# One Trainium2 core, a two-layer decoder trunk: the order of work at the norms, at the launch and at the start of the feed-forward output projection

## The chip, the cores and the metric

The kernel runs on 1 core of one Trainium2 chip. The metric is the device time of one execution in microseconds, the median of several runs. The program uses all five engines of the core: PE (TensorE matmul, with its weight loads PEld), DVE (VectorE), ACT (ScalarE), POOL (GpSimd) and SP (SyncE, which issues most DMAs).

## What is computed

256 tokens with 2048 features pass through two layers. Layer 0 has a mixer of a short convolution and a gated delta rule, layer 1 one of sparse attention; every mixer has an input projection ahead of it and an output projection (`w_out`, 2048 x 2048) behind it. The rest is the same in both layers:

```python
def swiglu_ffn(x, w_in, w_out):                     # FFN_HIDDEN = 5632
    gate, up = jnp.split(x @ w_in, 2, axis=-1)
    return (jax.nn.silu(gate) * up) @ w_out

def reference(x, ...):
    for i in range(DEPTH):                          # DEPTH = 2
        y = conv_deltanet_mixer(x, ...) if i % 2 == 0 else nsa_mixer(x, ...)
        x = layer_norm(DEEPNORM_ALPHA * x + y, ln_mix_g[i], ln_mix_b[i])
        x = layer_norm(DEEPNORM_ALPHA * x + swiglu_ffn(x, ffn_w_in[i], ffn_w_out[i]),
                       ln_ffn_g[i], ln_ffn_b[i])
    return x
```

So there are four norms. Norm 0 stands behind layer 0's mixer, norm 1 behind its feed-forward part, norms 2 and 3 likewise in layer 1. Everything is float32.

## The kernel before

**Precision.** Each float32 operand is split in two parts of a shorter format: `hi` is a copy by ACT (line 512 for weights, into `w_hi`), `lo` is the rest, a subtraction by DVE (line 947, into `w_lo`). A product is three matmuls (`passes`, lines 1570 to 1572): hi x hi, hi x lo, lo x hi. The 256 tokens are two tiles of 128, called tile 0 and tile 1 (`t`).

**Weights.** SP loads them in slabs of 1 MB (128 partitions x 2048) into four slots of `raw` (`RAW_SLOTS`). A slab is two halves of 128 x 1024; half `h` is split into slot `h % 4` of `w_hi` and `w_lo` (`HL_SLOTS` = 4). ACT splits half `h` when PE has used half `h - 4` (semaphore `half_used`), DVE follows ACT, and PE waits for `w_lo_ready`. In both queues a call `halves(n)` splits the next n halves; between these calls stands the rest of the engine's work, so the place of each call in the code sets the order. A half carries 12 matmuls of 512 columns in PE's work.

**Input projections** go chunk by chunk: 512 output columns, four slabs, two of the eight PSUM banks as accumulators, in alternating pairs (banks 0 and 1, banks 2 and 3). The feed-forward part has 22 such chunks, gates and ups in turn. The other four banks, 4 to 7, hold transposes. `up` (DVE, line 1119) multiplies gate and up into `hid`, `hidden_T` (PE, line 1747) transposes it, `put_hT` (ACT, line 620) copies it to `hT`.

**Output projections** (`outer`, in all three engines) use all eight banks as accumulators, 4 columns blocks x 2 tiles of tokens. They go over the k-tiles, 128 rows of the weight each: 16 for `out0` and `out1`, 44 for `fout0` and `fout1`. A k-tile needs two halves of weight and one column of the source, split into `a_hi` (ACT, line 543) and `a_lo` (DVE, line 993). Since every bank is needed from the first k-tile on, PE waits at the start of `fout` for the last `hid`, its transposes and their copies. The last two k-tiles are done bank by bank, first the four banks of tile 0, then those of tile 1, each reported by `bank_whole`.

**The norms** (`ln`). DVE adds each finished bank to `x` and takes its statistics (`moments`, lines 1013 and 1014), ACT takes the root (line 560), DVE inverts (lines 1022, 1027), ACT normalises `x` in two pieces of 128 x 1024 (line 567). PE transposes 512 features at a time (`x_tile_T`, line 1701; q is the quarter, 0 to 3), DVE scales quarters 0 and 2 (`turned_y`, line 1037), ACT quarters 1 and 3 (line 577); ACT splits off `xt_hi` (line 584), DVE `xt_lo` (line 1045, `turned_lo`). The next chunk, PE's `head`, can then begin: in it tile 0 takes the first two slabs alone, then tile 1, and the last two slabs go for both tiles together. The last norm (`last_ln`) writes its results to DRAM (lines 1092, 1093) and ends the program.

**The launch.** SP loads `x` (two tiles, 1 MB each), then the first slabs. PE turns `x` into x^T (`xT`, line 1582), 8 banks full of 4 transposes each through four banks, ACT and DVE split it (lines 530, 981), and then the first chunk, z0, begins.

Of the kernel before, what the change touches and what calls it, by code (L numbers as in the profile page):

```python
# [13 lines left out]
F32 = mybir.dt.float32  # L14
F32R = mybir.dt.float32r
# [61 lines left out]
def trunk(nc, x_in, positions, ln_mix_g, ln_mix_b, ln_ffn_g, ln_ffn_b, ffn_w_in, ffn_w_out,  # L77
          hy_w_in, sc_conv_w, dn_conv_w, dn_a_log, dn_dt_bias, dn_norm_w, hy_w_out,
          nsa_w_in, cmp_pos_k, cmp_w1_k, cmp_w2_k, cmp_pos_v, cmp_w1_v, cmp_w2_v, nsa_w_out,
          inv_freq, ln_by_feature, end_positions, out, stop=None):  # L80
# [3 lines left out]
    with ctx:  # L84
# [129 lines left out]

        bank = [ctx.enter_context(nc.psum_tensor(f"bank{n}", [P, 512], F32)) for n in range(8)]
# [13 lines left out]
        x_in_sem, small_in, nsa_in, w2_in = sem("x_in_sem"), sem("small_in"), sem("nsa_in"), sem("w2_in")  # L229
# [26 lines left out]
        uses([("xT", 0, u) for u in range(8)])  # L256
# [82 lines left out]
        def _(sp):  # L339
# [158 lines left out]
        def _(act):  # L498
            h_next = [0]

            def halves(count, i=None, per=0):

                for _ in range(count):
# [3 lines left out]
                    src, slot = half_of(h)  # L507
                    if h % 2 == 0:
                        act.wait_ge(slab_in[h // 2 % RAW_SLOTS], at(16 * (h // 2 // RAW_SLOTS + 1), i, 2 * per))
                    if h >= HL_SLOTS:  # L510
                        act.wait_ge(half_used, at(h - HL_SLOTS + 1, i, per))
                    act.activation(w_hi[:, slot, :], src, ACT.Copy).then_inc(w_hi_ready, 1)  # L512
# [12 lines left out]
            def split_xt(m):  # L525

                for q in range(4):
                    for u in (2 * q, 2 * q + 1):
                        wait_sp(act, ("xT", m, u))
                        ins = act.activation(xt_hi[:, 2 * u:2 * u + 2, :], sp_bank(("xT", m, u))[:, :].rearrange("p (a t) -> p a t", a=2),  # L530
                                             ACT.Copy)
                    ins.then_inc(xt_hi_ready, 1)

            def outer(name, n):
# [9 lines left out]

                def quad(kt, i=None):
                    for j in range(4):
                        if kt + j + 1 < n:
                            split(kt + j + 1, i)

# [1525 lines left out]
```

## Time and profile before

| | |
|---|---|
| median of 3 runs | 2611.42 us (2608.97 to 2611.67) |
| time of the profiled execution | 2611.9 us |
| span of the profiled execution, first to last instruction | 2610.1 us |
| PE busy, of the span | 2474.3 us, 95% |
| PEld / DVE / ACT busy | 81% / 56% / 44% |
| mean granted TensorE clock | 0.975 of full speed |

A row of a group gives the line, engine and operation, output<-inputs with their shape, the count, then busy time and the mean of one, then idle time before it and what ended it. A row of a timeline gives the start, the duration (of all that the row merges), the instruction, and in brackets the idle time before it. A window gives the busy time and count of each engine, then the granted clock as a share of full speed, which is 2.4 GHz; its lower level is 1.2 GHz. Matmuls overlap: one of 512 columns lasts 0.39 us and the next starts 0.23 us after it.

### The profile page before, as it was taken

How to read it: one execution, taken by the hardware profiler on the slowest of the kernel's cores; microseconds unless marked ns; L12 is line 12 of the kernel's file. 1: busy time of each engine (PE TensorE's matmuls, PEld its weight loads, DVE VectorE, ACT ScalarE, POOL GpSimd, SP SyncE). 2: the span in 40 equal slices, each digit the busy share in tenths (PEclk: the TensorE clock that was granted, in tenths of full speed). 3: DMA queues.
4: the chain of work that ended last, by engine and by line, in shares of the span. 5: the costliest groups of instructions: out<-in, count | busy, mean ns of one | idle time of the engine just before them, and what ended most of it. 6: DMA issues, size and time to landing. Idle time of an engine off the chain costs nothing. (4 is left out here: it accounts for less than half of the span.)

```text
span 2610.1 us, 33820 instructions
## 1 busy us (share of the span) xinstructions
PE 2474.3 (95%) x12841; PEld 2115.6 (81%) x12841; DVE 1452.5 (56%) x1791; ACT 1137.8 (44%) x1498; POOL 25.3 (1%) x71
## 2 busy tenths in 40 slices
PE   7999989888999999999979999979899999999997
PEld 6999979777888888788869877767688888878885
DVE  4666776566444444455567656645754444444556
ACT  4445542345444444444454445534544444444442
POOL 1000000100000000000000000000000000000000
PEclk9999999899999999999999999979999999999998
DMA  7555520344555555555535652215355555565552
GB/s 232 175 187 182 178 81 1 117 159 164 187 197 177 194 192 193 194 193 192 193 119 190 227 176 97 81 67 193 130 192 193 190 182 191 182 208 191 193 193 95
DMA packets 176306, 435.81 MB, mean 167 GB/s; under 512 B 7040, under 2 KB 19440, under 8 KB 159584
## 3 DMA queue, kind: packets, MB, share of 16 engines
q1 hardware_dynamic: 174496, 425.75, 48.7%
q0 software_dynamic: 1728, 8.92, 0.9%
q8 instruction: 57, 0.93, 0.1%
q14 instruction: 25, 0.20, 0.0%
HBM read 432.54 MB, written 2.10 MB: 167 GB/s over the span
## 5 line engine op out<-in xcount | busy, mean ns | idle before, releaser
L947 DVE TENSOR_TENSOR w_lo<-raw,w_hi 128x1024 fp32r<-128x1024 f32 x804 | 978.7, 1225 | 993.7 <-ACT w_hi L512 992.0
L512 ACT ACTIVATE w_hi<-raw 128x1024 fp32r<-128x1024 f32 x804 | 848.5, 1061 | 1130.5 <-PE bank L1572 1119.9
L1570 PE MATMUL bank<-w_hi,xt_hi 128*128 128x512 f32 x1728 | 683.6, 396 | 33.9 <-DVE xt_lo L1045 25.9
L1572 PE MATMUL bank<-w_hi,xt_lo 128*128 128x512 f32 x1728 | 676.8, 392 | 0.0
L1571 PE MATMUL bank<-w_lo,xt_hi 128*128 128x512 f32 x1728 | 676.8, 392 | 0.0
L1570 PEld LDWEIGHTS bank<-w_hi,xt_hi 128*128 128x128 f32 x1728 | 327.8, 190 | 102.2 <-DVE xt_lo L1045 27.3
L1570 PE MATMUL bank<-w_hi,a_hi 128*128 128x512 f32 x960 | 380.1, 396 | 17.1 <-DVE w_lo L947 9.6
L1572 PEld LDWEIGHTS bank<-w_hi,xt_lo 128*128 128x128 f32 x1728 | 327.0, 189 | 69.2
L1571 PEld LDWEIGHTS bank<-w_lo,xt_hi 128*128 128x128 f32 x1728 | 328.0, 190 | 66.9
L1571 PE MATMUL bank<-w_lo,a_hi 128*128 128x512 f32 x960 | 378.6, 394 | 0.0
L1572 PE MATMUL bank<-w_hi,a_lo 128*128 128x512 f32 x960 | 378.1, 394 | 0.0
L1570 PE MATMUL bank<-xt_hi,w_hi 128*128 128x256 f32 x928 | 266.9, 288 | 1.4 <-DVE w_lo L947 1.4
L1572 PE MATMUL bank<-xt_hi,w_lo 128*128 128x256 f32 x928 | 263.3, 284 | 0.0
L1571 PE MATMUL bank<-xt_lo,w_hi 128*128 128x256 f32 x928 | 263.2, 284 | 0.0
L1570 PEld LDWEIGHTS bank<-w_hi,a_hi 128*128 128x128 f32 x960 | 183.1, 191 | 58.0 <-DVE w_lo L947 11.3
L1572 PEld LDWEIGHTS bank<-w_hi,a_lo 128*128 128x128 f32 x960 | 183.4, 191 | 39.0
L1571 PEld LDWEIGHTS bank<-w_lo,a_hi 128*128 128x128 f32 x960 | 183.6, 191 | 38.3
L1570 PEld LDWEIGHTS bank<-xt_hi,w_hi 128*128 128x128 f32 x928 | 178.8, 193 | 3.9 <-DVE w_lo L947 2.3
L1571 PEld LDWEIGHTS bank<-xt_lo,w_hi 128*128 128x128 f32 x928 | 178.8, 193 | 2.0 <-issue 1.9
L1572 PEld LDWEIGHTS bank<-xt_hi,w_lo 128*128 128x128 f32 x928 | 178.7, 193 | 0.0
L993 DVE TENSOR_TENSOR a_lo<-big,a_hi 128x256 fp32r<-128x256 f32 x104 | 43.5, 418 | 6.6 <-ACT a_hi L543 6.6
L543 ACT ACTIVATE a_hi<-big 128x256 fp32r (+1 forms) x104 | 41.3, 400 | 0.2
(284 smaller groups left out, 1385.3 us busy)
## 6 DMA issues: line engine op xcount, KB each, us to landing
raw<-in_ffn_w_in_dram SPq DMA_DIRECT2D x176, 1024.0 KB, 5.0
raw<-in_ffn_w_out_dram SPq DMA_DIRECT2D x88, 1024.0 KB, 4.9
raw<-in_hy_w_in_dram SPq DMA_DIRECT2D x57, 1024.0 KB, 5.2
raw<-in_nsa_w_in_dram SPq DMA_DIRECT2D x41, 1024.0 KB, 5.1
raw<-in_hy_w_out_dram SPq DMA_DIRECT2D x16, 1024.0 KB, 4.8
raw<-in_nsa_w_out_dram SPq DMA_DIRECT2D x16, 1024.0 KB, 4.9
raw<-in_cmp_w_k_dram SPq DMA_DIRECT2D x4, 1024.0 KB, 6.0
raw<-in_cmp_w_v_dram SPq DMA_DIRECT2D x4, 1024.0 KB, 5.4
```

What stands on the lines that cost most here:

```text
L512: act.activation(w_hi[:, slot, :], src, ACT.Copy).then_inc(w_hi_ready, 1)
L543: act.activation(a_hi[:, kt % 4, :], s_, ACT.Copy).then_inc(a_hi_ready, 1)
L947: dv.tensor_tensor(w_lo[:, slot, :], src, w_hi[:, slot, :].bitcast(F32), ALU.subtract)\
L993: dv.tensor_tensor(a_lo[:, kt % 4, :], s_, a_hi[:, kt % 4, :].bitcast(F32), ALU.subtract)\
L1570: pe.matmul(dst, l_hi, r_hi, start=start, stop=False, skip_group_check=shared)
L1571: pe.matmul(dst, l_hi, r_lo, start=False, stop=False, skip_group_check=shared)
L1572: return pe.matmul(dst, l_lo, r_hi, start=False, stop=stop, skip_group_check=shared)
```

## The change

It has four parts. (1) **Launch**: a transposed copy of `x` comes in as an input of the program, `x_by_feature`, laid out in DRAM by the host, and is loaded in four quarters of 0.5 MB into `yt`, each ahead of the slab that needs it; ACT and DVE split it by quarters. The transposes of `xT` are gone, and `x` itself is loaded behind the slabs of z1. (2) **Norms**: at the end of every output projection tile 0 is three k-tiles ahead instead of two. Sixteen halves around each norm use eight slots rather than four: two groups of four lie in `spare_hi` and `spare_lo`, in a part of `big` that is free then. Three of the four transposes of tile 0 stand between tile 1's last banks, the next chunk does all four slabs for tile 0 and then all four for tile 1, and DVE's and ACT's orders follow. (3) **`fout`**: k-tiles 0 and 1 are first done for the four banks that are free already (`begin`), ahead of the last transposes, then for the other four. The splits of the source run two k-tiles ahead. (4) **Last norm**: DVE writes the first two results around tile 1's first bank. The accumulators are renumbered (`acc_bank`), and the last trip of DVE's feed-forward loop is written out.

```diff
-        HEAD = ("ffn0", "vs", "ffn1")
+        HEAD = ("ffn0", "vs", "ffn1", "fout1")
+        OUTER = (("out0", KT), ("fout0", FT), ("out1", KT), ("fout1", FT))
+        TAIL = 3
+        def acc_bank(n, t, c):
+            return pair(C[HEAD[n]] + t)[c] if c < 2 else bank[4 + 2 * t + c - 2]
         def turned_bank(n, t, q):
-            c = C[HEAD[n]]
-            return bank[4 + q] if t else pair(c + 1)[q % 2]
+            return acc_bank(n, 1, q) if t else acc_bank(n, 0, (2, 3, 1, 2)[q])
+        spared = {}
+        for n, (name, kts) in enumerate(OUTER):
+            for p in range(16):
+                spared[2 * (S[name] + kts) - (4 if n % 2 else 5) + p] = (int(n == 2), p)
+        def weights_of(h):
+            where, p = spared.get(h, (0, 4))
+            if p // 4 in (0, 2):
+                return spare_hi[where][:, p % 4, :], spare_lo[where][:, p % 4, :]
+            return w_hi[:, h % HL_SLOTS, :], w_lo[:, h % HL_SLOTS, :]
+        def slot_before(h):
+            if h in spared:
+                return h - 8 if spared[h][1] >= 4 else None
+            return h - HL_SLOTS if h >= HL_SLOTS else None
...
# SP: the launch
+            for quad in range(4):
+                v = slice(4 * quad, 4 * quad + 4)
+                sp.dma_start(yt[:, v, :], x_by_feature[:, v, :]).then_inc(xt_in[quad], 16)
+                slab(S["z0"] + quad, cols(w, quad, slice(6144, 6144 + CH)), as_in)
+            small("ba", w)
+            chunk(S["z1"], w, slice(6144 + CH, 6144 + 2 * CH))
             for t in range(NT):
                 sp.dma_start(x[:, t, :], x_in[0, t * P:(t + 1) * P, :]).then_inc(x_in_sem, 16)
...
# ACT: outer, ln, the end of ffn, the launch
+                ahead = 2 if name[0] == "f" else 1
...
             def ln(n):
+                halves(2)
                 root(n, 0)
+                halves(1)
                 normalise(n, 0)
                 act.wait_ge(gb_in, 48 * (n + 1))
-                halves(2)
+                halves(1)
                 turned_hi(n, 0, 0)
                 turned_hi(n, 0, 1)
+                halves(1)
+                turned_hi(n, 0, 2)
+                halves(1)
+                turned_hi(n, 0, 3)
+                halves(2)
                 root(n, 1)
-                halves(2)
-                turned_hi(n, 0, 2)
                 normalise(n, 1)
-                turned_hi(n, 0, 3)
...
+                def last_hT():
+                    halves(1)
+                    put_hT(k0 + 20, 40)
...
+                outer(f"fout{layer}", FT, last_hT)
...
+            for q in range(4):
+                act.wait_ge(xt_in[q], 16)
+                act.activation(xt_hi[:, 4 * q:4 * q + 4, :], yt[:, 4 * q:4 * q + 4, :], ACT.Copy).then_inc(xt_hi_ready, 1)
+                halves(2)
...
# DVE: last_ln, the end of ffn
                 inverse(n, 0)
                 result(0, slice(0, D // 2))
+                moments(n, 1, 0)
+                result(0, slice(D // 2, D))
                 for c in range(1, 4):
                     moments(n, 1, c)
-                result(0, slice(D // 2, D))
...
+                def last_up():
+                    up(c0 + 21, k0 + 20, False)
+                    mark().then_inc(gb_free, 1)
+                    halves(1)
+                outer(f"fout{layer}", FT, last_up)
...
# PE: outer's start and end, head
+                def begin(banks, last):
+                    for kt in range(2):
+                        pe.wait_ge(a_lo_ready, A0[name] + kt + 1)
+                        for hf in range(2):
+                            h = 2 * (S[name] + kt) + hf
+                            pe.wait_ge(w_lo_ready, h + 1)
...
+                if last_hidden:
...
+                    begin(free, False)
+                    last_hidden()
+                    pair_read(c - 1)
+                    sp_read(2)
+                    begin([b for b in bank if b not in free], True)
...
-                pe.wait_ge(w_lo_ready, h0 + 4)
                 for t in range(NT):
                     v = slice(t * P, (t + 1) * P)
+                    tile(n - TAIL, [t])
                     for c in range(4):
...
+                        if t and norm < 3:
+                            for q in {1: (0, 1), 2: (2,)}.get(c, ()):
+                                x_tile_T(norm, 0, q)
...
-                x_tile_T(n, 0, 0)
-                x_tile_T(n, 0, 1)
-                tokens_of(0, 0)
-                x_tile_T(n, 0, 2)
-                tokens_of(0, 1)
                 x_tile_T(n, 0, 3)
-                for q in range(4):
-                    x_tile_T(n, 1, q)
-                tokens_of(1, 0)
-                tokens_of(1, 1)
...
+                for quad in range(4):
+                    tokens_of(0, quad)
+                    if quad >= 2:
+                        x_tile_T(n, 1, 2 * quad - 4)
+                        x_tile_T(n, 1, 2 * quad - 3)
+                for quad in range(4):
+                    tokens_of(1, quad)
```

The order that this makes is shown at two places. The first is DVE at norm 0, from the first bank of tile 1 to the values by which tile 1 is normalised. Before, with `x<-x,bank` and `stats` being one bank's moments, `yt<-bank,lnT` a scaled quarter, `xt_lo` its lower part and `nmr` the value for the normalisation:

```order
L1013 SCALAR_TENSOR_TENSOR x<-x,bank 128x512
L1014 BN_STATS stats<-x 128x6
L1017 BN_AGGR mv<-stats 128x2
L1037 TENSOR_SCALAR yt<-bank,lnT 128x128 x4
L947 TENSOR_TENSOR w_lo<-raw,w_hi 128x1024
L1045 TENSOR_TENSOR xt_lo<-yt,xt_hi 128x4x128
L947 TENSOR_TENSOR w_lo<-raw,w_hi 128x1024
L1045 TENSOR_TENSOR xt_lo<-yt,xt_hi 128x4x128
L1022 RECIPROCAL rstd<-rstd 128x1
L1027 SCALAR_TENSOR_TENSOR nmr<-mv,rstd 128x1
```

These are its last rows, from tile 1's fourth bank on. The same stretch of the change, up to the same two rows at its end (the lines are those of the changed kernel):

```order
L1063 TENSOR_SCALAR yt<-bank,lnT 128x128 x4
L1039 SCALAR_TENSOR_TENSOR x<-x,bank 128x512
L1040 BN_STATS stats<-x 128x6
L980 TENSOR_TENSOR spare_lo_82<-raw,spare_hi_80 128x1024
L1071 TENSOR_TENSOR xt_lo<-yt,xt_hi 128x4x128
L1039 SCALAR_TENSOR_TENSOR x<-x,bank 128x512
L1040 BN_STATS stats<-x 128x6
L1043 BN_AGGR mv<-stats 128x2
L980 TENSOR_TENSOR spare_lo_82<-raw,spare_hi_80 128x1024
L1071 TENSOR_TENSOR xt_lo<-yt,xt_hi 128x4x128
L980 TENSOR_TENSOR spare_lo_82<-raw,spare_hi_80 128x1024
L980 TENSOR_TENSOR w_lo<-raw,w_hi 128x1024
L1048 RECIPROCAL rstd<-rstd 128x1
L1053 SCALAR_TENSOR_TENSOR nmr<-mv,rstd 128x1
```

Tile 1's third and fourth banks now stand between the quarters of tile 0, and four halves (`spare_lo`, `w_lo`) and two more `xt_lo` stand between the last bank and `nmr`, where two and two stood.

The second place is PE at the start of `fout0`, behind the last chunk of the feed-forward loop (banks and buffers numbered). Before, the transposes of `hid` come first:

```order
L1747 MATMUL bank6<-ident_60,yt_58 128x128 x4
L1747 MATMUL bank7<-ident_60,yt_58 128x128 x4
L1570 MATMUL bank0<-w_hi_50,a_hi_55 128x512
L1571 MATMUL bank0<-w_lo_51,a_hi_55 128x512
L1572 MATMUL bank0<-w_hi_50,a_lo_56 128x512
L1570 MATMUL bank4<-w_hi_50,a_hi_55 128x512
```

In the change these are the rows around the same transposes:

```order
L1608 MATMUL bank5<-w_hi_50,a_hi_55 128x512
L1609 MATMUL bank5<-w_lo_51,a_hi_55 128x512
L1610 MATMUL bank5<-w_hi_50,a_lo_56 128x512
L1808 MATMUL bank6<-ident_60,yt_58 128x128 x4
L1808 MATMUL bank7<-ident_60,yt_58 128x128 x4
L1608 MATMUL bank0<-w_hi_50,a_hi_55 128x512
```

Ahead of the transposes stand 24 matmuls on banks 2, 3, 4 and 5, of which the last three are shown, and behind them 24 on banks 0, 1, 6 and 7.

## Rows read from the trace of the kernel before

**Rows 1.** PE's waits, whole span: us in total, times, longest.
```profile
PE bank L1570 <- DVE xt_lo L1045: 25.9, 6, 4.4
PE bank L1570 <- DVE w_lo L947: 21.7, 11, 2.7
...
PE bank L1570 <- DVE a_lo L993: 7.5, 4, 1.9
```

**Rows 2.** Windows: us, busy time of each engine, granted clock, DMA share, GB/s.
```profile
0.00:15.00 15.00, 3.41 (x16) 3.20 (x16) 2.43 (x3) 4.07 (x4) 11.70 (x41) 1.00 0.88 328
15.00:23.00 8.00, 5.82 (x24) 5.34 (x25) 6.42 (x14) 5.55 (x10) 0.00 (x0) 0.57 1.07 309
...
561.00:621.00 60.00, 46.30 (x203) 37.57 (x202) 41.03 (x64) 31.86 (x47) 0.00 (x0) 0.94 0.38 126
1317.00:1379.00 62.00, 48.30 (x208) 39.12 (x208) 44.60 (x68) 32.09 (x47) 0.00 (x0) 0.92 0.36 118
...
1086.00:1106.00 20.00, 16.50 (x64) 13.05 (x63) 8.10 (x12) 7.22 (x11) 1.60 (x3) 0.83 0.68 243
```

**Rows 3.** PE's waits in the window 561 to 621 us, norm 0.
```profile
PE bank L1570 <- DVE xt_lo L1045: 8.6, 2, 4.4
PE bank L1570 <- DVE w_lo L947: 5.1, 2, 2.7
```

**Rows 4.** Timeline of the launch, PE and ACT.
```profile
8.87 3.41 PE L1582 MATMUL bank<-ident,x 128*128 128x128 f32 x16 [8.87 <-DMA x<-in_x_dram]
...
11.50 2.00 ACT L512 ACTIVATE w_hi<-raw 128x1024 fp32r<-128x1024 f32 x2 [9.40 <-DMA raw<-in_hy_w_in_dram]
...
20.51 0.77 PE L1570 MATMUL bank<-w_hi,xt_hi 128*128 128x512 f32 x1
```

**Rows 5.** Timeline of PE at norm 0: the first transposes.
```profile
580.04 1.03 PE L1701 MATMUL bank<-ident,x 128*128 128x128 f32 x8
```

**Rows 6.** Groups of DVE in the window 561 to 621 us: busy us, mean ns.
```profile
L947 DVE TENSOR_TENSOR w_lo<-raw,w_hi 128x1024 fp32r<-128x1024 f32 x14 | 17.0, 1223 | 7.3 <-ACT w_hi L512 7.2
L1014 DVE BATCH_NORM_STATS2 stats<-x 128x6 f32<-128x512 f32 x8 | 5.6, 695 | 0.3
L1045 DVE TENSOR_TENSOR xt_lo<-yt,xt_hi 128x512 fp32r<-128x512 f32 x8 | 5.4, 688 | 6.3 <-ACT xt_hi L584 6.3
L1013 DVE SCALAR_TENSOR_TENSOR x<-x,bank 128x512 f32<-128x512 f32 x8 | 5.4, 672 | 1.8 <-PE bank L1572 1.8
L1037 DVE TENSOR_SCALAR yt<-bank,lnT 128x128 f32<-128x128 f32 x16 | 5.3, 399 | 3.1 <-PE bank L1701 3.1
```

**Rows 7.** Groups of ACT in the window 561 to 621 us.
```profile
L512 ACT ACTIVATE w_hi<-raw 128x1024 fp32r<-128x1024 f32 x14 | 14.6, 1054 | 10.2 <-PE bank L1572 10.2
L577 ACT ACTIVATE yt<-bank,lnT 128x128 f32<-128x128 f32 x16 | 6.0, 452 | 1.8 <-PE bank L1701 1.8
L584 ACT ACTIVATE xt_hi<-yt 128x512 fp32r<-128x512 f32 x8 | 4.9, 628 | 6.8 <-DVE yt L1037 6.7
L567 ACT ACTIVATE x<-x,nmr,rstd 128x1024 f32<-128x1024 f32 x4 | 4.7, 1231 | 1.2 <-DVE nmr L1027 1.2
```

**Rows 8.** Timeline of the start of `fout0`: DVE, then PE, then ACT.
```profile
1082.43 1.23 DVE L947 TENSOR_TENSOR w_lo<-raw,w_hi 128x1024 fp32r<-128x1024 f32 x1 [1.49 <-ACT w_hi L512]
1085.15 1.23 DVE L947 TENSOR_TENSOR w_lo<-raw,w_hi 128x1024 fp32r<-128x1024 f32 x1 [1.49 <-ACT w_hi L512]
1087.00 1.29 DVE L1119 TENSOR_TENSOR yt<-bank,yt 128x512 f32<-128x512 f32 x2 [0.63 <-PE bank L1572]
...
1091.34 0.77 PE L1570 MATMUL bank<-w_hi,a_hi 128*128 128x512 f32 x1 [1.89 <-DVE a_lo L993]
...
1089.04 1.09 ACT L620 ACTIVATE big<-bank 128x512 f32<-128x512 f32 x2 [3.92 <-PE bank L1747]
```

**Rows 9.** Timeline of the end, PE and DVE.
```profile
2581.43 0.50 PE L1570 MATMUL bank<-w_hi,a_hi 128*128 128x512 f32 x1 [2.41 <-DVE w_lo L947]
...
2606.47 0.75 DVE L1093 SCALAR_TENSOR_TENSOR x<-x,rstd,gb 128x512 f32<-128x512 f32 x1
```

More of the change, by code:

```diff
@@ L523, in chunk_in, with outer @@
                 return pair(c)
-            def split_xt(m):
-                for q in range(4):
[L528 to L534, printed above, removed]
+            def outer(name, n, between=None):
                 src = outer_src(name)
@@ L543, in split @@
                     act.activation(a_hi[:, kt % 4, :], s_, ACT.Copy).then_inc(a_hi_ready, 1)
+                ahead = 2 if name[0] == "f" else 1
                 def quad(kt, i=None):
                     for j in range(4):
-                        if kt + j + 1 < n:
-                            split(kt + j + 1, i)
-                        halves(2 if kt + j < n - 2 or i is not None else n - 1 - kt - j, i, 8)
-                split(0)
+                        if kt + j + ahead < n:
+                            split(kt + j + ahead, i)
+                        halves(2 if kt + j < n - 2 or i is not None else (n - 1 - kt - j) * (ahead == 1), i, 8)
+                for kt in range(ahead):
+                    split(kt)
+                if ahead == 2:
+                    between()
                 loop_over(n // 4 - 1, 8, lambda i: quad(0, i))
@@ L994, in split @@
                       .then_inc(a_lo_ready, 1)
+                ahead = 2 if name[0] == "f" else 1
                 def quad(kt, i=None):
                     for j in range(4):
-                        if kt + j + 1 < n:
-                            split(kt + j + 1, i)
-                        halves(2 if kt + j < n - 2 or i is not None else n - 1 - kt - j, i, 8)
-                split(0)
+                        if kt + j + ahead < n:
+                            split(kt + j + ahead, i)
+                        halves(2 if kt + j < n - 2 or i is not None else (n - 1 - kt - j) * (ahead == 1), i, 8)
+                for kt in range(ahead):
+                    split(kt)
+                if ahead == 2:
+                    between()
                 loop_over(n // 4 - 1, 8, lambda i: quad(0, i))
@@ L1069, in ln @@
                 turned_lo(n, 0, 1)
+                turned_y(n, 0, 2)
+                moments(n, 1, 2)
+                halves(1)
+                turned_lo(n, 0, 2)
+                moments(n, 1, 3)
+                halves(1)
+                turned_lo(n, 0, 3)
+                halves(2)
                 scale(n, 1)
-                turned_y(n, 0, 2)
-                halves(2)
-                turned_lo(n, 0, 2)
-                turned_lo(n, 0, 3)
                 turned_y(n, 1, 0)
@@ L1684, in outer @@
                         for k in range(2):
-                            kt, slot = n - 2 + k, (h0 + 2 * k + hf) % HL_SLOTS
+                            kt, h = n - 2 + k, h0 + 2 * k + hf
+                            pe.wait_ge(w_lo_ready, h + 1)
                             pe.wait_ge(a_lo_ready, A0[name] + kt + 1)
-                            ins = passes(bank[4 * t + c][:, :], a_hi[:, kt % 4, v], a_lo[:, kt % 4, v],
-                                         w_hi[:, slot, cols], w_lo[:, slot, cols], False, k == 1)
+                            w = [part_[:, cols] for part_ in weights_of(h)]
+                            ins = passes(acc_bank(norm, t, c)[:, :], a_hi[:, kt % 4, v], a_lo[:, kt % 4, v],
+                                         *w, False, k == 1)
                             if t and c == 1 and k == 0:
```

162 lines of the change are left out of this document (76 added, 86 removed).

## The prediction, made before the change was run

> **What bounds the kernel now.** I read the waits of PE first, since PE is busy for 95% of the span and each engine behind it for 56% at most. Nearly all of what PE waits for outside the two mixers is in four kinds of places. In the whole span its longest sums are for `xt_lo`, for `w_lo` and for `a_lo` [rows 1]. In the window of norm 0 they are 8.6 us for `xt_lo` and 5.1 us for `w_lo`, 13.7 us together [rows 3]; norms 1 and 2 show the same two sums. The windows then show the clock [rows 2]: at norm 0 a granted mean of 0.94 over 60 us. At half speed such a stretch does half its work, so the time lost is the length times what is missing: 60 x 0.06 = 3.4 us (two dips of 3.4 us at 1.2 GHz, each costing 1.7). Norm 1 has 0.92 over 62 us, 5.1 us. Each dip begins behind a wait of PE. The launch is third: the first matmul of a chunk starts at 20.51 us [rows 4]. The start of `fout` is fourth, and the end fifth, where PE's last bank is followed by DVE alone until 2606.47 + 0.75 = 2607.2 us [rows 9].
>
> **Pace.** One half of weight is split every 2.72 us where nothing waits (1082.43 to 1085.15) [rows 8]; that is PE's time for 12 matmuls. Six, a bank with two k-tiles or a half for one tile of tokens, take 1.36 us, a k-tile 5.45 us.
>
> **Part 1, the launch.** Before, 2 MB of `x` have landed at 8.87 us and a third MB, the first slab, at 11.50 us: 2.63 us for a MB [rows 4]. Now the first slab stands behind 0.5 MB instead of 2, and lands 3.95 us earlier, at 7.55. ACT's half takes 1.05 us [rows 7], DVE's 1.22 [rows 6], and x^T's first quarter, which landed before, is split by then. The first matmul starts at about 9.95 us: **10.6 us earlier**. A quarter and a slab are 1.5 MB, 3.95 us of loading, for 5.45 us of PE, so I expect no later wait in z0. `x` itself, 5.3 us of loading, goes behind z1's slabs, and raw slots hold four slabs, 21.8 us of PE: nothing. The transposes' 32 matmuls are inside the 10.6. The clock is less plain. Before, a dip ran to about 22 us, mean 0.57 in the window from 15 to 23 [rows 2], of which 1.6 us hit z0: 0.8 us come back. But the first matmuls may now be slow themselves. The window from 0 to 15 us claims a granted 1.00 [rows 2], yet there 16 transposes took 3.41 us, 0.213 each [rows 4], and 8 of the same kind took 1.03 us, 0.129 each, at norm 0 [rows 5]. I believe the durations and charge z0 one dip, 1.7 us. The part is worth 10.6 + 0.8 - 1.7 = **9.7 us**. The Trainium skill (TensorE: Matmul & The Clock Gate, Part 1: The HAM clock gate) says that "the default state is throttled, and activity releases the throttle". By that rule the charge stands, by the window's 1.00 it would be nothing and the part worth 11.4; no row shows the clock directly before the first matmul.
>
> **Part 2, the norms.** I lay the engines' orders out by hand, time 0 being PE's end of the k-tile n - 4. Durations: a bank's `moments` 0.67 + 0.69, a half 1.22, four `yt` 1.6 busy but 1.3 in a run of them, `xt_lo` 0.69 [rows 6] (0.05 to 0.1 less from start to start); ACT's half 1.05, four `yt` 1.5, `xt_hi` 0.63, a piece of `x` 1.2 [rows 7]; a group of transposes 0.52 [rows 5].
> PE does k-tile n - 3 for tile 0 (2.7) and its four banks (8.2). DVE follows bank by bank, and with the aggregate, ACT's root and the inverse `nmr` is there at 10.7. ACT splits a half and normalises until 12.4 and 13.6. PE is at 13.7 when it has tile 1's second bank, so the first transposes don't wait. With two more banks and two more groups of transposes it is at 18.5, the start of the next chunk. The wait for `w_lo` at the last k-tile (2.4 of the 5.1 us) is gone, as no half there needs a slot that is in use.
> DVE gets tile 1's first bank at 12.5. From there its queue is full: bank, half, `yt`, bank, `xt_lo` to 18.2, just in time for the chunk. Half, `xt_lo`, `yt`, bank, half, `xt_lo` end at 24.4, where PE came at 24.0: a wait of 0.45. The last bank and another half end at 27.1, where PE came at 25.8: 1.35. PE then meets tile 1's transposes at 28.5. Until `nmr` DVE has done 4 banks (5.3), 6 halves (7.1), 2 `yt` (2.5), 4 `xt_lo` (2.5) and small ones (0.5), 17.9 us from 12.5, so 30.4, and ACT's piece ends at 31.7: 3.2. Behind slab 4 and the last transposes (36.5) tile 1's first `xt_lo` waits for a `yt` of quarter 2 that stands ahead of it in DVE's queue: 38.1, 1.6. Nothing waits after that. The sum is **6.6 us of waits for 13.7**; DVE is the bound here now. All of them look like smaller copies of the old ones (which were 2.4 to 4.4 us); I charge one dip of 1.7 us, behind the 3.2.
> Gains: norm 0, 13.7 + 3.4 - 6.6 - 1.7 = 8.8; norm 1, 13.7 + 5.1 - 8.3 = 10.5; norm 2 like norm 0, 8.8. Together **28.1 us**. The bounds: if no wait leads to a dip, 5.1 us more; if every norm keeps its dips and its waits are 3 us longer than laid out, about 14 less. DVE leaves the norm 8 us ahead of PE with four halves more in hand than before; the residual updates that follow cost it 2.4 us each, two halves for each, 4.9 of the 5.45 us that PE gives it. Nothing is charged.
>
> **Part 3, `fout`.** Before, PE waits 1.6 us for `hid` and 1.9 for `a_lo` (7.5 in four waits) [rows 1], and the window has 0.83 over 20 us, 3.4 us [rows 2]: 6.9 each. Now PE has 24 matmuls, 5.45 us, on free banks first. `up` (1.29) and the fourth half (1.22) [rows 8] fit in these. What is left: `a_lo` of k-tile 0 comes about 0.25 us behind the last chunk, since DVE's half of 1085.15 ends at 1086.38 [rows 8] and 0.4 follow; and the second four banks wait for ACT's two copies, 1.09 [rows 8], of which the first starts under the second group of transposes, so 0.85 stay. No dip. 6.9 - 1.1 = 5.8, less 0.1 for slower first matmuls: 5.7 each, **11.4 us**.
>
> **Part 4, the end.** PE's wait of 2.41 us ends at 2581.43 [rows 9]; less the k-tile of 5.45 time 0 is 2573.6, and DVE ends 33.6 later. In the new order tile 0's statistics end at 9.7, the inverse 0.65 later, the first result (two passes of 1.28) at 13.05, then bank, result, three banks, root (21.6) and four results of 1.45: 27.6. **6.0 us.**
>
> **The sum.** 9.7 + 28.1 + 11.4 + 6.0 = 55.2 us off the profiled execution's own time of 2611.9: **2556.7 us**. That execution stands 0.5 us above the median. A measurement of this kernel can tell about 0.2%, 5 us, from no change.
>
> **The rivals.**
> *The clock stays up.* None of the norms' waits brings a dip: 5.1 less, 2551.6 us. For it: the wait of 2.4 us at norm 0 brought none. Against: both of 4.4 did, and mine of 3.2 lies between. 0.15.
> *DVE holds the norms longer.* It has 17.9 us in a row, and ACT's order is fixed too; each item that comes late moves all behind it. With 3 us more per norm and the old number of dips (7 for 3, 6.8 us) it is 2556.7 + 9 + 6.8 = 2572.5. It decides if DVE's items cost 15% more than in the rows of before. 0.15.
> *The launch gains nothing.* The quarters and slabs share the queue badly and the first matmul stays at 20 us: 9.7 more, 2566. The rows speak against it, since DMA moved 328 GB/s there [rows 2]. 0.05.
> *Slower.* In `fout` the splits of the source now stand two k-tiles ahead, and the halves a half more. If that made one split of each k-tile late by a DVE half, 1.22 us, PE would lose it in 88 k-tiles: 107 us, 2664. It decides from 55.2 / 88 = 0.63 us per k-tile on. Against: a freed slot is split in 1.05 + 1.22 and two handovers, 2.5 us, and the half is due 8 us after it was freed. 0.03.
> The forecast has the rest, 0.62.
>
> **Range.** From 2547 us (no dips at the norms, none at the launch, 3 us to spare) to 2572 us, where DVE's case is half in. Faster 0.96, within 0.2% 0.01, slower 0.03.
>
> **What would show it.** PE's first matmul near 10 us; in the norm windows waits for `xt_lo` and `x` near 5 us and for `w_lo` near 1.4, and DVE without idle time for 18 us; at `fout` no wait over 1 us and a granted clock of 1.00; the last result 27.6 us behind k-tile n - 4. A first matmul after 13 us, waits of over 10 us at a norm, or new waits for `w_lo` in the long loops would make it wrong.

## The result, and the profile after

The changed kernel takes **2552.97 us** (median of 4 runs, 2552.24 to 2554.32), the kernel before 2611.55 us beside it (4 runs, 2608.97 to 2611.74). The ratio is 0.9779, with a 95% interval of 0.9762 to 0.9795. The forecast was 2556.7 us, 3.7 us too high. The profiled execution of the change took 2553.14 us, of which its span is 2551.4.

PE's waits over the whole span, after the change (columns as in [rows 1]: us in total, times, longest):

```profile
PE bank L1608 <- DVE w_lo L980: 14.6, 5, 10.4
...
PE bank L1768 <- ACT x L591: 8.2, 3, 2.7
PE bank L1608 <- DVE xt_lo L1071: 5.8, 6, 1.6
...
PE bank L1608 <- DVE a_lo L1015: 4.4, 4, 2.1
...
PE bank L1608 <- DVE spare_lo L980: 3.1, 3, 1.1
```

`xt_lo` has gone from 25.9 to 5.8 us. `w_lo` had 21.7 us in 11 waits; of its 14.6 us now, 10.4 are the launch (before, its longest wait was 2.7). In their place stand the normalised `x` of tile 1 with 8.2 and a half in the spare slots with 3.1 us, one wait at each norm.

To see where the time went, I take PE's start or end at the same matmul in both traces (an end is the last matmul's start plus PE's pace of 0.23 us):

| Place in the program | before | after | gained since the start |
|---|---|---|---|
| z0 ends | 43.17 | 34.43 | 8.74 |
| `out0` starts | 487.56 | 477.33 | 10.23 |
| the first chunk behind norm 0 ends | 620.56 | 600.79 | 19.77 |
| the last chunk ahead of `fout0` ends | 1086.58 | 1066.85 | 19.73 |
| k-tile n - 4 of `fout0` ends | 1317.30 | 1292.32 | 24.98 |
| the first chunk behind norm 1 ends | 1378.36 | 1341.07 | 37.29 |
| `out1` starts | 1745.02 | 1706.28 | 38.74 |
| the first chunk behind norm 2 ends | 1876.75 | 1829.62 | 47.13 |
| the last chunk ahead of `fout1` ends | 2342.78 | 2295.68 | 47.10 |
| k-tile n - 4 of `fout1` ends | 2573.43 | 2521.13 | 52.30 |
| the span ends | 2610.1 | 2551.4 | 58.7 |

So the launch gave 8.7 us, the norms 9.5, 12.3 and 8.4, the starts of `fout` 5.2 each, the end 6.4, and the two mixers, in which PE has the same matmuls as before, 1.5 each.

**The launch.** The eight groups of transposes of `x` are no longer in the timed program: the host lays the transposed copy out. ACT's timeline, then PE's (us from the span's start, duration, instruction, in brackets the wait before it):

```profile
7.97 2.00 ACT L541 ACTIVATE w_hi<-raw 128x1024 fp32r<-128x1024 f32 x2 [2.29 <-DMA raw<-in_hy_w_in_dram]
...
10.43 0.77 PE L1608 MATMUL bank<-w_hi,xt_hi 128*128 128x512 f32 x1 [10.43 <-DVE w_lo L980]
10.99 0.63 PE L1609 MATMUL bank<-w_lo,xt_hi 128*128 128x512 f32 x1
...
15.35 0.40 PE L1608 MATMUL bank<-w_hi,xt_hi 128*128 128x512 f32 x1
15.59 0.40 PE L1609 MATMUL bank<-w_lo,xt_hi 128*128 128x512 f32 x1
```

The first slab lands at 7.97 us, where 7.55 were forecast. Matmuls then start 0.43 us apart (10.99, 11.42, 11.85) until about 14.8, and 0.23 apart from there on: half speed for 4.4 us.

**The windows** at the launch and at norms 0, 1 and 2, then at the start of `fout0` (columns as in [rows 2]):

```profile
0.00:15.00 15.00, 4.57 (x11) 3.64 (x12) 6.79 (x7) 8.24 (x8) 12.59 (x30) 1.00 0.89 322
...
550.00:601.00 51.00, 45.25 (x205) 36.59 (x204) 36.04 (x60) 27.21 (x43) 0.00 (x0) 0.97 0.42 150
1292.00:1342.00 50.00, 44.27 (x211) 35.79 (x210) 41.46 (x65) 28.98 (x45) 0.00 (x0) 1.00 0.47 161
1779.00:1830.00 51.00, 45.26 (x205) 36.60 (x204) 35.90 (x60) 28.54 (x44) 0.00 (x0) 0.97 0.41 149
...
1066.00:1086.00 20.00, 18.99 (x87) 15.35 (x86) 10.79 (x15) 8.68 (x12) 1.59 (x3) 1.00 0.75 288
```

Before, the norms had a granted clock of 0.94 and 0.92 and the start of `fout0` 0.83 [rows 2]. Norms 0 and 2 now have one dip each (581.6 to 585.0 and 1810.4 to 1813.8), norm 1 and `fout0` none.
**Norm 0**, PE's timeline, the four places where it waits:

```profile
574.91 0.50 PE L1608 MATMUL bank<-spare_hi,xt_hi 128*128 128x512 f32 x1 [0.33 <-DVE xt_lo L1071]
...
577.62 0.50 PE L1608 MATMUL bank<-spare_hi,xt_hi 128*128 128x512 f32 x1 [1.05 <-DVE spare_lo L980]
...
582.02 1.97 PE L1768 MATMUL bank<-ident,x 128*128 128x128 f32 x8 [2.75 <-ACT x L591]
...
589.75 0.50 PE L1608 MATMUL bank<-w_hi,xt_hi 128*128 128x512 f32 x1 [1.62 <-DVE xt_lo L1071]
```

Counted as the delay of the next start against PE's own pace, these are 0.49, 1.21, 2.91 and 1.66 us, the same to 0.02 at all three norms; 0.45, 1.35, 3.2 and 1.6 were forecast. The transposes at 582.02 take 1.97 us where the same eight took 1.03 [rows 5]: the dip. DVE's timeline shows its queue from tile 1's first bank to the value for the normalisation:

```profile
563.06 0.69 DVE L1039 SCALAR_TENSOR_TENSOR x<-x,bank 128x512 f32<-128x512 f32 x1 [1.65 <-PE bank L1610]
...
580.34 0.15 DVE L1048 RECIPROCAL rstd<-rstd 128x1 f32<-128x1 f32 x1
580.53 0.16 DVE L1053 SCALAR_TENSOR_TENSOR nmr<-mv,rstd 128x1 f32<-128x1 f32 x1
```

It is 17.6 us long without a gap, from 12.4 to 30.1 us behind k-tile n - 4 (550.62). Forecast: 17.9 us, from 12.5 to 30.4. (Between tile 1's last bank and `nmr` stand three halves and one `xt_lo`, as the list of the changed order has it; the sentence below that list, which says four and two, counts from the third bank.)

**The start of `fout0` and the end**, PE's and DVE's timelines:

```profile
1067.23 0.47 PE L1608 MATMUL bank<-w_hi,a_hi 128*128 128x512 f32 x1 [0.22 <-DVE a_lo L1015]
...
1074.60 0.47 PE L1608 MATMUL bank<-w_hi,a_hi 128*128 128x512 f32 x1 [0.78 <-ACT big L648]
...
2548.22 0.75 DVE L1123 SCALAR_TENSOR_TENSOR x<-x,rstd,gb 128x512 f32<-128x512 f32 x1
```

Two short waits are left at `fout0`. DVE's last result ends at 2548.97, 27.84 us behind k-tile n - 4; 27.6 were forecast.

### The profile page after: what moved, and what is told of

It reads as the page before. It is cut to its first block, busy times and chain, and to the rows that moved or that the text cites. A ratio compares the mean times of both kernels' runs of the same rounds, so it can differ in the third digit from the quotient of the medians.

```text
span 2551.4 us, 33741 instructions
## 1 busy us (share of the span) xinstructions
PE 2450.6 (96%) x12809; PEld 2094.8 (82%) x12809; DVE 1448.5 (57%) x1783; ACT 1134.5 (44%) x1494; POOL 31.0 (1%) x71
## 4 chain that ended last, share of the span: by engine, by line
PE 89%; DVE 8%; ACT 2%; issue 1%; DMA 0%; DVEq 0%; SPq 0%; ACTq 0%
PE bank L1608 27%; PE bank L1609 27%; PE bank L1610 27%; PE bank L1872 3%; PE bank L2064 1%; PE bank L1808 1%; ACT gb L897 1%; DVE w_lo L980 1%; PE bank L2034 1%; DVE stats L1040 1%; PE bank L1861 1%; DVE spare_lo L980 1%; DVE sm L1524 0%; DVE x L1039 0%; DVE yt L1063 0%
## 5 line engine op out<-in xcount | busy, mean ns | idle before, releaser
L980 DVE TENSOR_TENSOR w_lo<-raw,w_hi 128x1024 fp32r<-128x1024 f32 x776 | 943.9, 1224 | 941.3 <-ACT w_hi L541 939.7
L541 ACT ACTIVATE w_hi<-raw 128x1024 fp32r<-128x1024 f32 x776 | 819.2, 1061 | 1064.6 <-PE bank L1610 1059.8
L1608 PE MATMUL bank<-w_hi,xt_hi 128*128 128x512 f32 x1680 | 661.0, 393 | 15.3 <-DVE w_lo L980 10.4
L1610 PE MATMUL bank<-w_hi,xt_lo 128*128 128x512 f32 x1680 | 655.7, 390 | 0.0
L1609 PE MATMUL bank<-w_lo,xt_hi 128*128 128x512 f32 x1680 | 655.5, 390 | 0.0
L1608 PEld LDWEIGHTS bank<-w_hi,xt_hi 128*128 128x128 f32 x1680 | 316.9, 189 | 80.9 <-issue 10.4
L1608 PE MATMUL bank<-w_hi,a_hi 128*128 128x512 f32 x896 | 351.1, 392 | 6.0 <-DVE a_lo L1015 4.4
L1609 PE MATMUL bank<-w_lo,a_hi 128*128 128x512 f32 x896 | 350.5, 391 | 0.0
L1610 PE MATMUL bank<-w_hi,a_lo 128*128 128x512 f32 x896 | 350.4, 391 | 0.0
L1609 PEld LDWEIGHTS bank<-w_lo,a_hi 128*128 128x128 f32 x896 | 169.3, 189 | 35.2
L1015 DVE TENSOR_TENSOR a_lo<-big,a_hi 128x256 fp32r<-128x256 f32 x104 | 43.3, 418 | 13.7 <-ACT a_hi L563 13.7
L639 ACT ACTIVATE yt<-bank 128x512 f32<-128x512 f32 x44 | 23.9, 597 | 43.6 <-PE bank L1610 43.6
```

The source lines that it names most:

```text
L541: act.activation(weights_of(h)[0], half_of(h), ACT.Copy).then_inc(w_hi_ready, 1)
L980: dv.tensor_tensor(lo, half_of(h), hi.bitcast(F32), ALU.subtract).then_inc(w_lo_ready, 1)
L1015: dv.tensor_tensor(a_lo[:, kt % 4, :], s_, a_hi[:, kt % 4, :].bitcast(F32), ALU.subtract)\
L1608: pe.matmul(dst, l_hi, r_hi, start=start, stop=False, skip_group_check=shared)
L1609: pe.matmul(dst, l_hi, r_lo, start=False, stop=False, skip_group_check=shared)
L1610: return pe.matmul(dst, l_lo, r_hi, start=False, stop=stop, skip_group_check=shared)
```

## Experiments

A ratio is against the kernel before, run on the same chip, with its 95% interval. The kernel before took 2609.9, 2609.6 and 2610.3 us (medians) in the three series.

### Which part gives what

**The launch alone.** The kernel before, with the change's launch only:

```
+            for q in range(4):
+                act.wait_ge(xt_in[q], 16)
+                act.activation(xt_hi[:, 4 * q:4 * q + 4, :], yt[:, 4 * q:4 * q + 4, :], ACT.Copy).then_inc(xt_hi_ready, 1)
+                halves(2)
```

> The kernel before with the new launch alone. If the parts are independent and only waits and dips of the clock count, chunk z0 ends 8.7 us earlier, as in the change, and the whole execution is 8.7 us faster (about 2603 us), give or take one or two dips of the clock in the first mixer (1.7 us each), in which the change itself was 1.5 us faster though nothing is edited there. The rival says that the 1.5 us in the mixer come with the launch (x out of the way of the first slabs, another order of loads): then this kernel shows them too, 10.2 us in all at the start of out0.

Measured: 2601.96 us (2596.03 to 2602.53, 6 runs), ratio 0.9968 [0.9955, 0.998], 7.9 us less by the medians. The trace is of the fastest execution, 2596.03 us, while the other five took 2600.4 to 2602.5. In it z0 ends at 33.55 us, 9.6 earlier than before, and `out0` starts 11.5 earlier. The waits for `xt_lo` and `a_lo` are those of before, and those for `w_lo` too, less the launch (10.3):

```profile
PE bank L1575 <- DVE w_lo L950: 31.9, 12, 10.3
PE bank L1575 <- DVE xt_lo L1048: 25.8, 6, 4.4
...
PE bank L1575 <- DVE a_lo L996: 7.5, 4, 1.9
```

So the launch stands by itself and the norms' gain owes nothing to it. Layer 0's mixer takes 1.9 us less here than before and layer 1's 3.8, and no edit accounts for either; the section on the prediction comes back to this.

**`fout`: transposes first, then the free banks.** Only the place of one call differs from the change; the splits stay two k-tiles ahead:

```
-                    begin(free, False)
                     last_hidden()
                     pair_read(c - 1)
                     sp_read(2)
+                    begin(free, False)
                     begin([b for b in bank if b not in free], True)
```

> The change, but in fout PE does the last transposes first and then the same matmuls on the four free banks. The source's first two k-tiles are still split ahead. If the 24 matmuls ahead of the transposes are what hides the chain, PE waits about 1.8 us for hid and 0.8 us for ACT's copies, 2.6 us instead of 1.2, and 1.7 to 3.4 us more from a dip of the clock behind it: 3 to 5 us per fout, 6 to 10 us in all, 2559 to 2563 us. The rival says that splitting the source ahead is what does it (before, the wait for a_lo was the longer one): then it is 1.4 us per fout and no dip, 2556 us.

Measured: 2557.33 us (2556.48 to 2559.73), ratio 0.9799 [0.9782, 0.9815], between what the theory (2559 to 2563) and the rival (2556) expected. PE's waits at `fout0` in this kernel, then the window of `fout1`:

```profile
PE bank L1808 <- DVE yt L1150: 1.8, 1, 1.8
PE bank L1608 <- ACT big L648: 0.8, 1, 0.8
```

```profile
2296.00:2310.00 14.00, 11.46 (x47) 8.99 (x46) 4.12 (x8) 3.23 (x6) 1.58 (x3) 0.88 0.70 290
```

In the trace this costs 1.45 us at `fout0`, where no dip follows, and 3.08 us at `fout1`, where one does (2300.7 to 2304.1). So the rival's 1.4 us came true at `fout0` and the theory's 3 to 5 us at `fout1`. The 24 matmuls ahead of the transposes hide 1.5 us, and 1.6 more where their absence brings a dip. By difference the rest of the 5.2, 3.8 us at `fout0` and 2.1 at `fout1`, belongs to what this kernel keeps. In it the wait for `a_lo` behind the transposes (1.9 us) is gone, ACT's copies (0.8) have appeared, and of the 6.8 us at the lower clock that each start had before, none is left at `fout0` and 3.4 at `fout1`. So most of that rest is dips that don't come, with the splits two k-tiles ahead as the likely reason. Those splits were not run alone.

**The norms: tile 0 two k-tiles ahead, not three.** `tile(n - 3)` is done for both tiles together:

```
-        TAIL = 3
+        TAIL = 2
...
                 tile(n - 4, range(NT))
+                tile(n - 3, range(NT))
...
-                    tile(n - TAIL, [t])
```

> The change with tile 0 two k-tiles ahead instead of three. By the hand-laid schedule the first transposes of tile 0 now wait about 1.6 us for the normalised x in each of three norms, of which 0.6 us is won back from the later wait for w_lo, since DVE is the bound from then on: 0.9 us more per norm, and at the end DVE starts 2.7 us later and ends 2.7 us later: 5.5 us slower in all, about 2558.5 us. The rival says that the third k-tile is what made the norm faster: then it would be over 3 us per norm and over 12 us in all.

Measured: 2556.16 us (2554.56 to 2556.68), ratio 0.9793, 3.2 us over the change. PE's waits at norm 0:

```profile
PE bank L1768 <- ACT x L591: 4.3, 2, 2.8
PE bank L1608 <- DVE xt_lo L1071: 1.6, 1, 1.6
PE bank L1608 <- DVE spare_lo L980: 1.0, 1, 1.0
```

The first transposes now wait 1.66 us for the normalised tile 0, which they did not before, and 0.49 goes: 1.2 us more per norm, where 0.9 was expected. The wait of 2.9 us for tile 1 stays. From k-tile n - 4 to the end it is 32.99 us and not 30.27, the 2.7 us expected. The third k-tile is thus worth 1.2 us at a norm and 2.7 at the end. These make 6.3 us, and the median shows 3.2, the expectation being 5.5: the dips fell otherwise than in the change (none at norms 0 and 2, one at norm 1, so 1.7 us less), and layer 1's mixer, which this edit doesn't touch, took 1.8 us less in the trace.

**The last norm in its old order on DVE.** Both results of tile 0 and the sums of tile 1 as before:

```
-                result(0, slice(0, D // 2))
                 moments(n, 1, 0)
-                result(0, slice(D // 2, D))
+                result(0, slice(0, D // 2))
                 for c in range(1, 4):
                     moments(n, 1, c)
+                result(0, slice(D // 2, D))
```

> The change with the old order of DVE in the last norm. By hand, tile 1's first bank was complete 0.7 us before the first result ends in the new order; in the old order DVE would wait for it: statistics of tile 0 end at 9.7 us behind k-tile n - 4, the bank is complete at 12.3, so DVE idles about 2 us. 2 us slower, about 2555 us. If the new order does nothing, because DVE's work is the same, it is within 0.5 us.

Measured: 2556.44 us (2548.57 to 2558.82), ratio 0.9783 [0.9765, 0.9802]. The runs lie 10 us apart, so the median can't tell. The trace, which is of the slowest of them, can: the end is 31.55 us behind k-tile n - 4, 1.3 us more, since DVE now waits for a bank:

```profile
2538.05 0.69 DVE L1039 SCALAR_TENSOR_TENSOR x<-x,bank 128x512 f32<-128x512 f32 x1 [1.83 <-PE bank L1610]
```

Two were expected. Of the 6.4 us at the end, 1.3 are this order's, 2.7 the third k-tile's; the other 2.4 weren't tested apart.

**The change again.**

> The change itself once more, beside the next three on the same chip. Every theory expects the time seen before, 2553 us within 2 us, and the waits of the norms to the tenth: 0.5, 1.2, 2.9, 1.7 us. The dips of the clock may differ: the same wait of 2.9 us had a dip behind it at norms 0 and 2 and none at norm 1.

Measured: 2552.87 us (2551.77 to 2557.29), ratio 0.9786. Every mark of the table above is met within 0.1 us, and the dips fall at the same places.

### What the clock does at the launch

**46 transposes of the identity ahead of z0**, into a bank that nothing reads:

```
+            pe.wait_ge(ident_ready, 1)
+            for _ in range(46):
+                pe.transpose(bank[4][:, 0:P], ident[:, :], ident[:, :])
             chunk(S["z0"], C["z0"], True, m=0)
```

> The change with 46 transposes of the identity on PE ahead of the first chunk, from about 1.5 us on, into a bank that nobody reads. If the clock is low at the launch because PE did nothing before, the matmuls of z0 start 0.23 us apart from the first one on, instead of 0.43 for 4.4 us: z0 ends 2.1 us earlier, the whole 2551 us. The rival says that those matmuls are slow for another reason at the launch (DMA traffic at 400 GB/s beside them, first use of the code): then they stay 0.43 us apart, or z0 ends 0 to 1 us later.

Measured: 2551.48 us (2550.61 to 2553.54), ratio 0.9776. PE's timeline and the window behind it:

```profile
1.59 6.67 PE L1826 MATMUL bank<-ident 128*128 128x128 f32 x46 [1.59 <-POOL ident L463]
10.57 0.47 PE L1608 MATMUL bank<-w_hi,xt_hi 128*128 128x512 f32 x1 [2.30 <-DVE w_lo L980]
10.87 0.39 PE L1609 MATMUL bank<-w_lo,xt_hi 128*128 128x512 f32 x1
```

```profile
10.00:15.00 5.00, 4.43 (x13) 3.52 (x14) 4.61 (x5) 3.96 (x5) 4.61 (x7) 0.66 1.05 399
```

The transposes start 0.213 us apart at first and 0.109 from the 15th on, and the first matmuls behind them 0.23, so PE was at half speed in the change for want of earlier work. The rival, DMA traffic or the first use of the code, would have left them 0.43 apart; here the traffic is the same (399 GB/s). Then, after 2.3 idle us, the clock falls all the same (0.66 of full in that window), and z0 ends only 0.36 us earlier. The median meets the 2551 us expected, but not for the reason given: the 2.1 us at z0 did not come. The Trainium skill (TensorE: Matmul & The Clock Gate, Part 1: The HAM clock gate) says that "the default state is throttled, and activity releases the throttle"; these rows agree, 0.43 us apart without earlier work and 0.23 with it.

### Moving what DVE and ACT do at the norms

DVE is the bound in a norm, so the question is which of its waits are its load and which its order.

**Tile 1's statistics earlier.** DVE scales ahead of the last two halves, ACT normalises between them:

```
# DVE
+                scale(n, 1)
                 halves(2)
-                scale(n, 1)
...
# ACT
-                halves(2)
                 root(n, 1)
+                halves(1)
                 normalise(n, 1)
+                halves(1)
```

> The change with nmr of tile 1 made ahead of the last two halves in DVE's queue, and ACT's root likewise. If DVE's full queue is what PE waits for, the wait of 2.9 us for the normalised x shrinks to about 0.85 and one of 1.0 us for w_lo appears in the fourth slab: 1.4 us less per norm, and no dip behind it, so 4 us plus up to 3.4 us faster: 2546 to 2549 us. The rival, that ACT's order holds the norm, expects the wait of 2.9 us to stay over 2 us.

Measured: 2548.07 us (2545.79 to 2548.22), ratio 0.9761 [0.9745, 0.9777]. PE's waits at norm 0:

```profile
PE bank L1609 <- DVE xt_lo L1072: 1.9, 2, 1.6
PE bank L1609 <- DVE spare_lo L981: 1.1, 1, 1.1
PE bank L1609 <- DVE w_lo L981: 0.9, 1, 0.9
PE bank L1769 <- ACT x L591: 0.5, 1, 0.5
```

The wait for `x` falls from 2.9 to 0.65 us against the pace, and one of 1.02 for the half that now comes later appears. The granted clock is 1.00 at all three norms. In the trace they gain 6.1 us together (2.5, 1.1 and 2.5), while z0 and layer 0's mixer take 1.5 longer with no edit there.

**Two other moves.** The third half ahead of tile 1's first sums, and tile 1's first `xt_lo` ahead of a later quarter:

```
-                moments(n, 1, 0)
                 halves(1)
+                moments(n, 1, 0)
...
                 turned_y(n, 1, 0)
+                turned_lo(n, 1, 0)
                 turned_y(n, 1, 2)
-                for q in range(4):
+                for q in range(1, 4):
```

> The change with two other items of DVE's queue moved: the third half ahead of tile 1's first bank (DVE idles there for 1.8 us), and tile 1's first xt_lo ahead of its scaled quarter 2. By the hand-laid schedule the wait of 1.7 us at tile 1's first slab goes to nothing and the one of 0.5 us too, while the 2.9 us stays, since everything ahead of nmr moves together with PE's tokens: 2.1 us less per norm, 6.4 us in all, about 2546.5 us. If the waits only move to another place, the time stays at 2553 us.

Measured: 2543.58 us (2543.03 to 2545.92), ratio 0.975 [0.9734, 0.9766]. PE's waits at norm 0:

```profile
PE bank L1769 <- ACT x L591: 2.7, 1, 2.7
PE bank L1609 <- DVE spare_lo L980: 1.0, 1, 1.0
```

The waits of 0.49 and 1.66 us for `xt_lo` are gone. Every norm has its dip (0.97 in each window), and the kernel is 9.4 us faster than the change where 6.4 were expected. Not all of that is the edit's: in the trace the three norms gain 5.5 us, layer 1's mixer 2.7 and `out1` 0.8, with no edit in these two.

**All three moves.** With ACT splitting one half, taking the root, splitting the other, then normalising.

> The change with the three moves in DVE's queue together: third half ahead of tile 1's first bank, nmr ahead of the last two halves (and ACT's root between them), tile 1's first xt_lo ahead of the scaled quarter. By hand the waits per norm are 1.2 us for w_lo in the third slab, 0.85 for the normalised x and nearly nothing else, 2.1 instead of 6.3 us; with no dip at the norms 3 x 4.2 + 3.4 = 16 us faster than the change at most, 12.5 at least: 2537 to 2540.5 us. If DVE's total of 17.9 us decides whatever the order, it stays at the 2543.6 us of the kernel with two of the moves.

Measured: 2535.43 us (2533.46 to 2538.5, 5 runs), ratio 0.9712 [0.9698, 0.9725]. PE's waits at norm 0, and the windows of the norms:

```profile
PE bank L1610 <- DVE spare_lo L981: 1.0, 1, 1.0
PE bank L1770 <- ACT x L591: 0.5, 1, 0.5
```

```profile
540.00:600.00 60.00, 58.45 (x272) 47.80 (x271) 46.31 (x70) 38.47 (x57) 0.00 (x0) 1.00 0.49 174
1270.00:1330.00 60.00, 58.47 (x273) 47.78 (x272) 48.29 (x72) 37.91 (x55) 0.00 (x0) 1.00 0.50 176
1750.00:1815.00 65.00, 63.48 (x294) 51.92 (x294) 49.20 (x73) 40.96 (x59) 0.00 (x0) 1.00 0.51 177
```

DVE does the same work, and 4.4 of the change's 6.3 us of waits per norm are gone with it: most of them were order, not load. No norm has a dip. In the trace the norms gain 17.0 us (6.1, 4.7 and 6.1), where 16 were expected at most.

**The same, and 62 transposes ahead of z0**, enough of them to reach to the first matmul.

> The same with 62 transposes of the identity at the launch, which last until the first half is split; with 46 PE had 2.3 us of idle time left and the dip came 1 us behind it. If idle time alone brings dips, the first chunk now runs at 0.23 us a matmul throughout and ends 2 us earlier: 2 us faster than the kernel without them. If the transposes do not count as work for the clock, the dip stays and nothing is gained.

Measured: 2534.17 us (2531.89 to 2536.38), ratio 0.9705 [0.9692, 0.9719]. PE's timeline, and the window of z0:

```profile
1.59 9.81 PE L1828 MATMUL bank<-ident 128*128 128x128 f32 x62 [1.59 <-POOL ident L463]
11.16 0.48 PE L1610 MATMUL bank<-w_hi,xt_hi 128*128 128x512 f32 x1
11.47 0.40 PE L1611 MATMUL bank<-w_lo,xt_hi 128*128 128x512 f32 x1
```

```profile
11.00:33.00 22.00, 22.00 (x100) 18.25 (x99) 14.82 (x13) 12.54 (x12) 8.40 (x18) 1.00 1.06 357
```

The transposes hold the first matmul back by 0.86 us, but z0 then takes 21.9 us and not 24.7, and ends 2.0 earlier, as expected. Of that pair the kernel without them has the longest z0: the nine traces with the new launch and no transposes take 23.3 to 24.7 us for it and end it between 33.6 and 35.0, so the gain over them is 0.5 to 2.0 us. By the medians the two kernels differ by 1.3 us, within what a measurement can tell.

**`fout`'s second four banks in two pairs.** Banks 0 and 1 need only the end of the last chunk, banks 6 and 7 ACT's copies:

```
-                    begin(free, False)
+                    begin(free, {})
                     last_hidden()
                     pair_read(c - 1)
+                    begin(pair(c - 1), {(0, 0): 1})
                     sp_read(2)
-                    begin([b for b in bank if b not in free], True)
+                    begin([b for b in bank if b not in free and b not in pair(c - 1)], {(0, 1): 2, (1, 1): 1})
```

> The same again, and in fout the second round of four banks is split in two: banks 0 and 1, which up has read, come directly behind the transposes, banks 6 and 7, which ACT's copies must clear, 2.7 us later. The wait of 0.83 us in each of two fout goes: 1.7 us faster. If the release of the halves, which now comes later for three of four, makes w_lo late in k-tile 2, the gain is lost to a wait there.

Measured: 2528.96 us (2526.02 to 2532.02, 5 runs), ratio 0.9688 [0.9675, 0.9701]. The stretch from the last chunk to k-tile 2 is 1.0 us shorter at each `fout`, 2.1 in all where 1.7 were expected; of its waits one is left, that for `a_lo`:

```profile
PE bank L1610 <- DVE a_lo L1016: 0.2, 1, 0.2
```

This is the fastest version: 24 us under the change and 81 under the kernel before. Of the 5.2 us that the medians put it under the last kernel, the edit explains 2.1. In the traces the two mixers took 4.1 us less, with no edit in them.

## Why the prediction was right, and where its sizes were off

The forecast case came true. Of its 55.2 us the spans show 58.7 (2610.1 - 2551.4). The four parts that it sums give 55.7 of these, and the closeness is partly luck: they miss by 1.0 too much, 2.1 too little, 1.0 too much and 0.4 too little. The other 3.0 us are in the mixers.

- **Launch: 9.7 forecast, 8.7 measured.** The step that was off is the landing of the first slab, 7.97 us and not 7.55. It was priced at the pace of 2.63 us per MB that the rows showed behind 2 MB, here behind the first 0.5. The rest is the slow start, 2.1 us and not 1.7. Neither is a fixed size: over the twelve traces with this launch the slab lands between 7.59 and 8.07 us, and over the nine without transposes z0 ends 8.2 to 9.6 us earlier than before. That there would be one, against the window's 1.00, was right, and the warm transposes show why.
- **Norms: 28.1 forecast, 30.2 measured.** The waits were laid out at 6.6 us and came to 6.3, each within 0.3. The term that was off is the count of dips, one for each norm: norm 1 had none, which makes it 12.3 and not 10.5. The sum also takes its 13.7 us of before from the view's idle time and its 6.6 as delays of the next start; in the view's idle time the waits at norm 0 are now 5.8, so 7.9 us and a dip went, 9.6, where 8.8 were forecast and 9.5 came. And 60 x 0.06 is 3.6 as it stands there; the 3.4 that it uses is right, two dips of 3.4 us at half speed. At norm 2 the last three k-tiles and the chunk gained 9.1 (1876.75 - 1817.47 against 1829.62 - 1779.48), about as at norm 0 (9.4); its 8.4 from `out1`'s start contain 0.75 lost within the loop. The rival of a DVE that is 15% slower did not occur: 17.6 us for 17.9.
- **Starts of `fout`: 11.4 forecast, 10.4 measured.** The waits were 0.38 and 0.83 (0.25 and 0.85 forecast), and no dip came. The sum was near, 1.0 us too high. Most of that is the old dip: it ran from 1090.5 to 1097.4 us, and PE stood idle in it until 1091.34, so it cost 3.0 us and not 3.4. What I took for the mechanism, the matmuls ahead of the transposes, is worth 1.5 of the 5.2 us at `fout0` and 3.1 at `fout1`, where without them a dip came.
- **End: 6.0 forecast, 6.4 measured.** DVE ended 27.84 us behind k-tile n - 4, not 27.6, and before it was 33.8 (2607.2 - 2573.43), not 33.6: 5.95 for 6.0. The other 0.45 lie behind DVE's end, where the span went on for 2.9 us before and 2.4 now.
- **Mixers: nothing forecast, 3.0 measured.** The windows of the two mixers before, then after:

```profile
43.17:487.56 444.39, 418.67 (x3264) 400.45 (x3262) 299.76 (x430) 185.93 (x221) 1.35 (x3) 0.98 0.38 127
1378.36:1745.02 366.66, 336.79 (x1980) 294.22 (x1979) 229.87 (x388) 172.39 (x360) 3.06 (x5) 0.94 0.40 134
...
34.43:477.33 442.90, 416.87 (x3264) 398.50 (x3262) 299.67 (x430) 185.93 (x221) 1.35 (x3) 0.98 0.38 132
1341.07:1706.28 365.21, 333.91 (x1980) 291.74 (x1979) 230.04 (x389) 172.42 (x360) 3.06 (x5) 0.95 0.39 132
```

PE's instructions there are the same in number, and their busy time is 1.8 and 2.9 us less. The time at the lower clock is less too: 18.7 us for 21.7 in layer 0's, 35.9 for 41.0 in layer 1's. It is not a gain to count on. Over the twelve traces of changed kernels, all with the same matmuls there, layer 0's mixer takes 442.5 to 444.1 us and layer 1's 362.6 to 366.7, and the kernel with all three moves, at 444.1 and 366.7, has next to nothing of it. So it goes with where the dips fall. Why they fall where they do was not tested.

- **The slower rival** (a split late in each k-tile of `fout`, 107 us) was wrong: from k-tile 2 to k-tile n - 4 `fout0` takes 212.2 us before and after, so nothing is lost in these k-tiles.

What stays open: whether the new order of the norms would give as much with four weight slots. It was not tried, since tile 0 there needs eight halves before any is freed. So of the largest part, the 30.2 us at the norms, only the third k-tile (1.2 us a norm) and the three later moves are tested one by one; slots, PE's order and DVE's are not told apart. Nor are the splits ahead in `fout`, or 2.4 us at the end.

## What to carry to other kernels

Where one engine holds the others up, lay its queue out by hand, instruction by instruction, with durations from the trace: that gave every wait within 0.3 us, and it shows which item stands in front of one that somebody waits for. Moving three such items took another 17.5 us off the change without a single instruction less. And test the parts of a change one by one even where its sum comes out right: here the free banks, which I took for what makes `fout` start faster, gave 1.5 of 5.2 us at one start and 3.1 at the other. Compare traces stretch by stretch as well, since two of them can differ by 2 to 4 us in stretches that no edit touches.

## What was unexpected of the hardware

- **The same wait brings a dip or not.** The wait of 2.9 us, equal to 0.01 at the three norms, is followed by 3.4 us at 1.2 GHz at norms 0 and 2 and by none at norm 1, twice alike. With one k-tile less ahead it is the other way round. A wait of 2.3 us at the launch brought one too. So did waits of 1.9 and 0.9 us at `fout1`, where the same two at `fout0` brought none. The wait's length alone does not foretell a dip here.
- **Runs of one kernel differ by it.** The kernel with the old last norm ran between 2548.6 and 2558.8 us; its mean granted clock was 0.986 in the fastest and 0.982 in the slowest.
- **Work that nobody reads counts.** Transposes of the identity into an unread bank bring PE to its higher clock before the first real matmul: they start 0.213 us apart at first and 0.109 later, and the first matmuls then 0.23 us apart, not 0.43.
